# First feed-forward of a two-block transformer kernel: wide products for the first two chunks

## The reference, cut to what matters

```python
def conv_ffn(h, w_up, conv_w, conv_b, w_down):
    S = h.shape[1]
    u = jnp.einsum('bsd,df->bsf', h, w_up)                 # 1024 -> 2 * 2816
    up = jnp.pad(u, ((0, 0), (CONV_WIDTH - 1, 0), (0, 0)))
    u = conv_b + sum(conv_w[j] * up[:, j:j + S] for j in range(CONV_WIDTH))
    gate, val = u[..., :D_FF], u[..., D_FF:]
    return jnp.einsum('bsf,fd->bsd', jax.nn.silu(gate) * val, w_down)

x = x + conv_ffn(rms_norm(x, ffn_norm_w), w_up, conv_w, conv_b, w_down)
```

## Time and profile before

| | |
|---|---|
| median of 3 runs | 805.94 us (805.93 to 806.11) |
| profiled execution | 805.84 us, of which its span 804.0 us |
| PE busy | 799.2 us (99%) in 4860 matmuls |
| PEld busy | 690.4 us (86%) |
| DVE busy | 591.2 us (74%) in 920 instructions |
| ACT busy | 472.5 us (59%) in 692 instructions |
| chain that ended last | PE 96%, DVE 2%, DMA 1%, SP queue 1% |

### The profile page before, as it was taken

How to read it: one execution, slowest core, us unless ns; L and a number is a source line. 1 busy time by engine, 2 the same in 40 slices (tenths; PEclk the granted TensorE clock), 3 DMA queues, 4 the chain that set the end, 5 groups by cost and what they waited for, 6 DMA issues and landing times.

```text
span 804.0 us, 12564 instructions
## 1 busy us (share of the span) xinstructions
PE 799.2 (99%) x4860; PEld 690.4 (86%) x4860; DVE 591.2 (74%) x920; ACT 472.5 (59%) x692; POOL 42.6 (5%) x88
## 2 busy tenths in 40 slices
PE   9999999999999999999999999999999999999998
PEld 8878889888888888888888889999998888888886
DVE  6897789987878888677988863686576755566654
ACT  6876456655665666867566555655844744444442
POOL 0000000000000000003242510100000000000000
PEclk9999999999999999999999999999999999999999
DMA  9943344664665563654454463334365656655551
GB/s 329 357 166 106 106 157 158 209 210 159 207 205 174 195 234 135 240 168 158 172 183 159 156 208 107 105 107 147 125 201 161 182 182 209 208 175 191 172 193 53
DMA packets 90351, 142.08 MB, mean 177 GB/s; under 512 B 3840, under 2 KB 56768, under 8 KB 90176
## 3 DMA queue, kind: packets, MB, share of 16 engines
q1 hardware_dynamic: 89728, 140.38, 52.4%
q10 hardware_dynamic: 576, 1.05, 0.4%
HBM read 140.37 MB, written 1.05 MB: 176 GB/s over the span
## 4 chain that ended last, share of the span: by engine, by line
PE 96%; DVE 2%; DMA 1%; SPq 1%; issue 0%
PE bank L511 22%; PE bank L512 21%; PE bank L513 21%; PE bank L600 14%; PE bank L605 8%; PE bank L382 3%; PE bank L1121 1%; PE bank L1144 1%; DMA vec<-in_vectors 1%; PE bank L1057 1%; PE bank L584 1%; DVE w_lo L1779 1%; SPq L413 0%; PE bank L587 0%; PE bank L742 0%; PE bank L1081 0%
## 5 line engine op out<-in xcount | busy, mean ns | idle before, releaser
L1779 DVE TENSOR_TENSOR w_lo<-raw,w_hi 128x1024 fp32r<-128x1024 f32 (+1 forms) x254 | 302.0, 1214 | 59.2 <-ACT w_hi L1271 58.6
L1271 ACT CAST w_hi<-raw 128x1024 fp32r<-128x1024 f32 (+1 forms) x254 | 260.1, 1045 | 114.4 <-PE bank L513 111.6
L511 PE MATMUL bank<-w_hi,h_both 128*128 128x512 f32 (+1 forms) x336 | 133.5, 397 | 0.1
L512 PE MATMUL bank<-w_lo,h_both 128*128 128x512 f32 (+1 forms) x336 | 130.4, 388 | 0.0
L513 PE MATMUL bank<-w_hi,h_both 128*128 128x512 f32 (+1 forms) x336 | 130.4, 388 | 0.0
L600 PE MATMUL bank<-a_both,w_hi 128*128 128x512 f32 x512 | 121.5, 389 | 0.0
L600 PEld LDWEIGHTS bank<-a_both,w_hi 128*128 128x128 f32 x512 | 95.5, 188 | 19.4
L511 PE MATMUL bank<-w_hi,a_both 128*128 128x512 f32 (+1 forms) x270 | 106.4, 394 | 0.0
L512 PE MATMUL bank<-w_lo,a_both 128*128 128x512 f32 (+1 forms) x270 | 104.9, 388 | 0.0
L513 PE MATMUL bank<-w_hi,a_both 128*128 128x512 f32 (+1 forms) x270 | 104.8, 388 | 0.0
L511 PEld LDWEIGHTS bank<-w_hi,h_both 128*128 128x128 f32 x336 | 63.3, 188 | 14.8 <-issue 2.4
(11 more groups left out here) (235 smaller groups left out, 1057.2 us busy)
## 6 DMA issues: line engine op xcount, KB each, us to landing
raw<-in_w_in SPq DMA_DIRECT2D x45, 1024.0 KB, 5.1
raw<-in_w_up SPq DMA_DIRECT2D x22, 1024.0 KB, 5.0
raw<-in_w_ff_up SPq DMA_DIRECT2D x16, 1024.0 KB, 5.4
raw<-in_w_ff_down SPq DMA_DIRECT2D x16, 1024.0 KB, 4.8
raw<-in_w_down SPq DMA_DIRECT2D x11, 1024.0 KB, 4.9
raw<-in_w_out SPq DMA_DIRECT2D x8, 1024.0 KB, 5.0
raw<-in_w_gla_branch SPq DMA_DIRECT2D x4, 1024.0 KB, 5.0
raw<-in_w_attn_branch SPq DMA_DIRECT2D x2, 1024.0 KB, 5.0
```

The source lines that it names most:

```text
L511: nc.tensor.matmul(dst, l_hi, r_hi, start=start, stop=False)
L512: nc.tensor.matmul(dst, l_hi, r_lo, start=False, stop=False)
L1271: nc.scalar.copy(dst, raw_half(m % RAW, half, size, cols)).then_inc(s.hi_done, 1)
L1779: nc.vector.tensor_tensor(dst, raw_half(n // 2 % RAW, n % 2, size, cols), h, ALU.subtract).then_inc(s.lo_done, 1)
```

## The change

The products of the first two chunks use `wide_columns` in place of three narrow matmuls for each depth tile; the helper `up_part` goes. ACT copies the low-half columns of the banks for these two chunks as it does for the later ones. `up_sum` on DVE waits for that copy, adds the first half of the bank to it and, for the first two chunks, multiplies the sum in place by `rms_row` in a second instruction, linked to the first.

```diff
-            def up_part(n, acc, ks):
-                q = n % RING
-                pe.wait_ge(s.lo_done, n + 1)
-                for k in ks:
-                    ins = passes(acc[:, 0:TOKENS], w_hi[:, q, k * P:(k + 1) * P], w_lo[:, q, k * P:(k + 1) * P],
-                                 h_hi[:, k, :], h_lo[:, k, :], k == 0, k == KT - 1)
-                if k == KT - 1:
-                    ins.then_inc(s.mm_done, 1)
...
-            up_part(n1, bank[:, 0, :], low)
-            up_part(n1 + 1, bank[:, 1, :], low)
+            wide_columns(n1, bank[:, 0, :], ks=low)
+            wide_columns(n1 + 1, bank[:, 1, :], ks=low)
...
-            up_part(n1 + 3, bank[:, 3, :], range(KT))
+            wide_columns(n1 + 3, bank[:, 3, :], ks=range(KT))
             for f in range(4):
                 if f % 2 == 0:
                     pe.wait_ge(s.ffn_summed, f // 2 + 1)
-                up_part(n1 + 4 + f, bank[:, f, :], range(KT))
+                wide_columns(n1 + 4 + f, bank[:, f, :], ks=range(KT))
...
             def ff1_chunk(j, e, mm, split1, split2, split3):
-                if mm is not None:
-                    up_copy(e, 0, mm)
+                up_copy(e, 0, mm)
                 split1()
                 act.wait_ge(s.ffn_summed, j * 2 + 1)
                 taps(j, e, 0)
-                if mm is not None:
-                    up_copy(e, 1, mm + 2)
+                up_copy(e, 1, mm + 2)
                 split2()
...
-            ff1_chunk(0, 0, None, lambda: hi(n1 + 5), lambda: (scaled_hi(0), hi(n1 + 6, n1 + 7)), lambda: hi(n1 + 8))
-            ff1_chunk(1, 1, None, lambda: (scaled_hi(1), hi(n1 + 9)), lambda: hi(n1 + 10, n1 + 11, n1 + 12, n1 + 13),
+            ff1_chunk(0, 0, n1 + 2, lambda: hi(n1 + 5), lambda: (scaled_hi(0), hi(n1 + 6, n1 + 7)), lambda: hi(n1 + 8))
+            ff1_chunk(1, 1, n1 + 6, lambda: (scaled_hi(1), hi(n1 + 9)), lambda: hi(n1 + 10, n1 + 11, n1 + 12, n1 + 13),
                       lambda: None)
...
             def up_sum(j, e, v):
+                dve.wait_ge(s.ffn_low, j * 2 + v + 1)
+                u = up1[:, v, e, :].rearrange("p (f t) -> p f t", f=2)
+                ins = nc.vector.tensor_tensor(u, bank[:, 2 * v:2 * v + 2, 0:TOKENS], u, ALU.add)
                 if isinstance(j, int) and j < 2:
-                    dve.wait_ge(s.mm_done, 2 * M_FF1 + 4 * j + 2 * v + 2)
-                    nc.vector.tensor_tensor(up1[:, v, e, :].rearrange("p (f a t) -> p f a t", f=2, a=TT),
-                                            bank[:, 2 * v:2 * v + 2, 0:TOKENS].rearrange("p f (a t) -> p f a t", a=TT),
-                                            rms_row.rearrange("p (o a t) -> p o a t", o=1, a=TT).to_broadcast([P, 2, TT, P]),
-                                            ALU.mult).then_inc(s.ffn_summed, 1)
-                    return
-                dve.wait_ge(s.ffn_low, j * 2 + v - 3)
-                u = up1[:, v, e, :].rearrange("p (f t) -> p f t", f=2)
-                nc.vector.tensor_tensor(u, bank[:, 2 * v:2 * v + 2, 0:TOKENS], u, ALU.add).then_inc(s.ffn_summed, 1)
+                    link(ins)
+                    ins = nc.vector.tensor_tensor(u, u, rms_row.rearrange("p (o t) -> p o t", o=1).to_broadcast([P, 2, TOKENS]),
+                                                  ALU.mult)
+                ins.then_inc(s.ffn_summed, 1)
```

More of the change, by code:

```diff
@@ L900, in _ @@
             pe.wait_ge(s.h_lo_done, 6)
-            up_part(n1, bank[:, 0, :], low)
-            up_part(n1 + 1, bank[:, 1, :], low)
+            wide_columns(n1, bank[:, 0, :], ks=low)
+            wide_columns(n1 + 1, bank[:, 1, :], ks=low)
             turn_half(1, 1)
             pe.wait_ge(s.acc_free1, 5)
-            up_part(n1 + 2, bank[:, 2, :], low)
+            wide_columns(n1 + 2, bank[:, 2, :], ks=low)
             pe.wait_ge(s.h_lo_done, 8)
-            up_part(n1, bank[:, 0, :], high)
-            up_part(n1 + 1, bank[:, 1, :], high)
+            wide_columns(n1, bank[:, 0, :], ks=high)
+            wide_columns(n1 + 1, bank[:, 1, :], ks=high)
             pe.wait_ge(s.ffn_rms, 1)
@@ L913, in _ @@
             ins.then_inc(s.ffn_row, 1)
-            up_part(n1 + 2, bank[:, 2, :], high)
+            wide_columns(n1 + 2, bank[:, 2, :], ks=high)
             pe.wait_ge(s.ffn_row_in, 1)
-            up_part(n1 + 3, bank[:, 3, :], range(KT))
+            wide_columns(n1 + 3, bank[:, 3, :], ks=range(KT))
             for f in range(4):
```

## The result

The changed kernel takes 808.43 us (median of 8 runs, 808.30 to 808.46) against 805.93 us for the kernel before (8 runs, 805.81 to 806.11): 1.0029 times as long, 95% interval 1.0021 to 1.0038. It is 2.5 us slower; the forecast was 808.3.

A forecast was written before the change was run, and what follows sets the result against it. PE was taken as the bound, with DVE about half a microsecond ahead. Longer DVE sums of 2.84 us, less 0.11, less lead 0.42, plus 0.16 restart, add 2.47 to 805.84: 808.3 us, range 807.2 to 809.0.

The forecast's parts named there:

- DVE's lead: First two chunks' down products: DVE ends low parts only 0.54, 0.42 and 0.42 us before PE starts n1+8, n1+9, n1+14.
- The longer sum: DVE's half-chunk sum in the first two chunks: add, link and multiply take 1.31 in place of 0.60 us, four times.
- The sum of the terms: Lateness of PE's start of n1+14: 2.84 added, less 0.11, less 0.42, plus 0.16, makes 2.47 us.
- the lead of 0.42: Before the change, n1+14's first low part ends on DVE at 155.09 and PE starts on it at 155.51.
- the start after the stall: PE resuming after waiting for DVE: 0.06 us to wake and 0.10 in the first step, 0.16 in all.
- The three waits: PE waits for DVE's low parts of n1+8, n1+9 and n1+14: about 1.6, 0.7 and 0.5 us.
- What PE saves: First two chunks' up products: 0.346 in place of 0.360 us a depth tile, 0.86 us in all, lost in stalls.
- it waits for nobody: PE before the change, 114.75 to 155.50 us: busy throughout both stages, with no wait for another engine.
- ACT's copy in front of the splits: Chunk 0's value-half copy, queued before the splits of n1+6 and n1+7: hidden by 1.1 us, because DVE is late.
- the third rival: ACT's queue is the later one, copies delaying splits past their cover, or the sum costs 0.88: 809.0 and above; 8%.
- That the extra work vanishes in DVE's waits: First rival: DVE's 1.78 us of waits for ACT absorb the longer sums, 806.5 or 805.0 us, no change; 12%.
- The durations' 11.3 us: Second rival: matmul durations are the price, 177 ns saved a tile, 11.3 us in all, 794.5; 2%.

The follow-up runs named there:

- the last run: Changed kernel with moved splits, chunk 0's two multiplies on GpSimd, each beside a DVE rescale, chunk 1's on DVE: 805.13 us, 0.9990 times the kernel before.
- the moved splits: Changed kernel with the same instructions, splits of n1+8, n1+14 and n1+9 moved earlier in ACT's and DVE's queues: 805.67 us, 0.9997 times the kernel before.

## Why the prediction was right

**DVE's lead decides.** Right, and shown from five sides: the longer sums alone make the loss, without them it is gone, half of them make less than half of it, twice as many make it grow by all that is added, and the same work in another order makes none.

**The longer sum.** Forecast 1.31 us from its start to the next instruction's; measured 124.13 to 125.46, 1.33. The link starts its instruction 0.04 us after the end of the one before, where neighbours without one overlap by 0.08. The sentence of the Trainium skill that a semaphore "costs nothing extra" ("VectorE: DVE Perf Modes", section "The DRAIN you can't avoid") would have given a step of 1.20 and 807.9; 1.33 and 808.43 are with the rows.

**The sum of the terms** came out closer than its terms did. Forecast were 2.84 us of longer sums, less 0.11 by which DVE starts sooner, less the lead of 0.42, plus 0.16 for the start after the stall: 2.47. In the traces they are 2.92 (four times 0.73), 0.26 (118.95 to 118.69), 0.42 and 0.22 (0.15 to the start, 0.07 in the first step): 2.46. The agreement to 0.01 is luck. Of the 0.26, 0.19 is there when the stage begins, so the changed products give 0.07:

```profile
114.56 1.18 PE L584 MATMUL bank<-h_both,w_hi 128*128 128x512 f32 x4
...
118.69 0.69 DVE L2014 TENSOR_TENSOR h_both<-bank,h_both 128x512 fp32r<-128x512 f32 x1 [0.70 <-ACT h_both L1414]
```

In the kernel before PE begins the stage at 114.75. In the traces of all these kernels, the turn of activations just ahead of that point starts between 114.18 and 114.54, so 0.19 is within the spread of the traces.

**The three waits.** Low parts forecast to end at 139.71, 143.29 and 157.82 ended at 139.61, 143.21 and 157.75. PE waited 1.46, 0.51 and 0.48 us where 1.6, 0.7 and 0.5 were named, and started n1+14 at 157.90 with the next step 0.30 instead of 0.23 us behind; 157.98 in effect was forecast.

**What PE saves** was given too much, without effect on the sum. Forecast 0.86 us; in the last run, where PE does not wait, it goes from its first wide matmul (114.62) to n1+8 (138.18) in 23.56 us, against 24.19: 0.63 us. A full half-slab takes 2.79 us (126.96 to 129.75), not 2.77: a wide matmul takes 0.230 us in its run of eight (126.96 to 128.80) where the forecast took 0.227 from chunk 2's run of sixteen, which makes 0.2 us over 64 tiles. Why it is 0.230 is not shown. And one of the six parts of four tiles saves nothing: from 118.05 to 119.70 before and from 117.79 to 119.44 after it takes 1.65 us, because what follows it starts 0.06 us after DVE has made the next activations (119.64 and 119.38). So "it waits for nobody" was not quite right even before the change: these waits are too short to show as idle time.

**ACT's copy in front of the splits**, costed at nothing "only because DVE is late": right on both counts, and the third rival fell with it. It cost nothing in the changed kernel, where DVE starts n1+6 at 130.76 without a wait, and 0.3 us once the multiply was taken out. The expectation for that run had the copy only as a rival of 807.5 us or more and nothing for it in its own sum, and missed by 0.37 us.

**The rivals.** That the extra work vanishes in DVE's waits fell: those waits moved along with DVE (0.69, 0.26 and 0.69 us after). They can be used, but only by putting other work into them, as the moved splits show. The durations' 11.3 us did not come; starts are what counts.

## What to carry to other kernels

An engine at 99% on the path may have another one half a microsecond ahead of it. Before work is moved onto that one, subtract the end of each of its deliveries from the start of the user: what fits in the smallest of these leads is free, and everything past it costs its full length for good if the path has no slack behind. Where work has to be added, first look for gaps in the order of the queue (here 1.6 us in waits for an answer from ACT), and look whether the delivery wanted first is also made first.

## What was not expected of the hardware

A multiply of 128x512 on GpSimd took 1.29 to 1.30 us beside a rescale on DVE, which has one operand in PSUM. Beside DVE instructions with both operands in SBUF it took 1.48 us once (the taps) and 2.20 twice (the subtractions of 128x1024). The profile's spans of GpSimd are rough; DVE's own are the surer sign: all three groups with both operands in SBUF took 1.0 to 1.1 us longer, and the rescale stayed at 1.2. The Trainium skill, "SBUF — State Buffer", section "Who interferes with whom", says that a DVE instruction with two SBUF inputs contends with a GpSimd instruction that reads SBUF, and one with at most one such input, outside the 2-port perf modes, does not; these runs agree (1.04, 1.09 and 1.08 us longer with two SBUF inputs, nothing with one). Here GpSimd helped DVE only where it stood beside work that reads PSUM.
